# The start of a memory pool moves to a multiple of 256 bytes in a decoder-layer kernel

## The reference, cut to what matters

```
x = x + 0.5 * rmsnorm(swiglu_ffn(rmsnorm(x), w_gu1, w_down1))        # hidden width 2816
u = rmsnorm(x) @ w_in                                                 # four parts of 512
c  = silu(rmsnorm(causal_dwconv31(u_val * sigmoid(u_glu))))
yb = rg_lru(causal_dwconv4(u_x)) * gelu(u_gelu)
x = x + rmsnorm(concat(c, yb) @ w_out)
x = x + 0.5 * rmsnorm(swiglu_ffn(rmsnorm(x), w_gu2, w_down2))
x = x + rmsnorm(sigmoid(rmsnorm(x) @ ple_w_gate) * (p @ ple_w_proj))
```

## Time and profile before

| | |
|---|---|
| median of 3 runs | 2107.99 us (2106.99 to 2108.95) |
| span of the profiled execution, first to last instruction | 2105.4 us (its own time isn't listed) |
| instructions | 34,476, of them 13,041 matmuls |
| busy: TensorE, VectorE, ScalarE, GpSimd | 98%, 56%, 32%, 3% of the span |
| granted TensorE clock, mean | 0.998 |
| moved by DMA | 116.17 MB, 55 GB/s over the span |

### The profile page before, as it was taken

One profiled execution on the slowest core, in us unless ns is written; L12 is line 12 of the kernel. 1 busy time (PEld: TensorE's weight loads), 2 busy tenths in 40 slices (PEclk: granted clock), 3 DMA queues, 4 the chain that ended last, 5 costly groups with the idle time before them and its releaser, 6 DMA issues. The chain is left out here.

```text
span 2105.4 us, 34476 instructions
## 1 busy us (share of the span) xinstructions
PE 2065.3 (98%) x13041; PEld 2049.7 (97%) x13041; DVE 1188.6 (56%) x2367; ACT 681.6 (32%) x1401; POOL 71.7 (3%) x110
## 2 busy tenths in 40 slices
PE   7999999999999999999999999999999999999998
PEld 7999999999999998999999999999999999999997
DVE  5643544354435579537886855345544554358877
ACT  4321222122212234316774532212121222124555
POOL 0000000000000002321000000000000000000000
PEclk9999999999999999999999999999999999999999
DMA  5171111011101102332121211011101110021213
GB/s 166 61 106 35 60 60 40 20 60 60 43 17 60 60 1 50 67 58 50 45 82 61 80 61 61 10 50 60 60 16 44 60 60 30 29 80 41 61 41 103
DMA packets 153277, 116.17 MB, mean 55 GB/s; under 512 B 72648, under 2 KB 143628, under 8 KB 153200
## 3 DMA queue, kind: packets, MB, share of 16 engines
q1 hardware_dynamic: 117728, 108.41, 16.8%
q10 hardware_dynamic: 33424, 5.67, 2.0%
q0 software_dynamic: 2048, 1.06, 0.3%
HBM read 105.96 MB, written 9.15 MB: 55 GB/s over the span
## 5 line engine op out<-in xcount | busy, mean ns | idle before, releaser
L852 PE MATMUL ps<-x_hi,w_lo 128*128 128x352 f32 x2688 | 884.3, 329 | 6.9 <-DVE w_lo L2118 3.0
L854 PE MATMUL ps<-x_hi,w_hi 128*128 128x352 f32 x2688 | 869.7, 324 | 0.0
L853 PE MATMUL ps<-x_lo,w_hi 128*128 128x352 f32 x2688 | 865.2, 322 | 0.0
L852 PEld LDWEIGHTS ps<-x_hi,w_lo 128*128 128x128 f32 x2688 | 505.9, 188 | 10.1 <-issue 4.5
L853 PEld LDWEIGHTS ps<-x_lo,w_hi 128*128 128x128 f32 x2688 | 509.5, 190 | 0.0
L854 PEld LDWEIGHTS ps<-x_hi,w_hi 128*128 128x128 f32 x2688 | 506.4, 188 | 0.0
L852 PE MATMUL ps<-a_hi,wd_lo 128*128 128x352 f32 x1104 | 358.1, 324 | 6.5 <-DVE a_lo L2223 3.7
L854 PE MATMUL ps<-a_hi,wd_hi 128*128 128x352 f32 x1104 | 357.6, 324 | 0.0
L853 PE MATMUL ps<-a_lo,wd_hi 128*128 128x352 f32 x1104 | 355.6, 322 | 0.0
L2271 DVE TENSOR_TENSOR acc<-ps,acc 128x352 f32<-128x352 f32 x480 | 249.7, 523 | 88.7 <-PE ps L854 80.6
L2206 DVE TENSOR_TENSOR tmp_u<-ps,rstd_pre 128x352 f32<-128x352 f32 x132 | 69.0, 524 | 342.0 <-PE ps L854 342.0
(11 more groups left out here) (226 smaller groups left out, 1567.7 us busy)
## 6 DMA issues: line engine op xcount, KB each, us to landing
raw<-in_ffn_w_gu_dram SPq DMA_DIRECT2D x88, 512.0 KB, 3.5
rawd<-in_ffn_w_down_dram SPq DMA_DIRECT2D x22, 1024.0 KB, 7.3
raw<-in_w_in_dram SPq DMA_DIRECT2D x16, 512.0 KB, 4.0
raw<-in_w_out_dram SPq DMA_DIRECT2D x16, 512.0 KB, 4.0
raw<-in_ple_w_gate_dram SPq DMA_DIRECT2D x16, 512.0 KB, 4.0
toeplitz<-rev ACTq DMA_DIRECT2D x8, 512.0 KB, 8.3
x_in<-in_x_prompt_dram SPq DMA_DIRECT2D x4, 512.0 KB, 10.0
toep_first<-toeplitz SPq DMA_DIRECT2D x32, 64.0 KB, 2.2
```

The source lines that it names most:

```text
L852: eng.matmul(dst, wl, xh, start=first, stop=False)
L853: eng.matmul(dst, wh, xl, start=False, stop=False)
L854: return eng.matmul(dst, wh, xh, start=False, stop=last)
```

## The change

One line: the pool's start, and with it the running offset, is rounded up to the next multiple of 256 bytes. Sizes, order, engines and queues are untouched.

```
         st_out = tile("st_out", [P, NJ, 36])
-        pool0 = at[0]
+        pool0 = at[0] = (at[0] + 255) // 256 * 256

         acc = tile("acc", [P, KT, TOK])
```

## The result

The kernel after takes 2093.53 us (median of 7 runs, 2090.77 to 2102.49), the kernel before beside it 2108.95 us: a ratio of 0.9929, 95% interval [0.9909, 0.9949]. That is faster by 0.7%, where no change was forecast, and more than the largest gain for which the prediction had a price. The profiled spans are 2105.4 and 2091.4 us, 14.0 us apart. Of the seven executions of either kernel two took some 10 us longer than the rest (2118.9 us before, 2102.0 and 2102.5 after), so the medians and the profiles are those of the majority. The instructions, their order and their queues are the same; 44 tiles stand 32 bytes further on.

The account below looks back on a forecast made before the run. TensorE bounds the kernel: number of matmuls times 160 to 161 ns, plus some tens of us of waits. Matmuls, VectorE and ScalarE, and transfers were each taken as 0, giving 2108.0 us, range 2104.5 to 2111.5.

Parts of the forecast that it names:

- Two placements, one pace, chunk by chunk, to 0.2 ns: Feed-forward loop matmuls: activations and tokens, placed differently, both run at 160 to 161 ns, so moving the pool gains 0.
- The bound of 4.2 us: Most the matmuls could gain: 2.3 us from 3312 activation matmuls at the third chunk's pace, 1.9 us from output projection.
- The closing caveat: Prediction fails if pace depends on an address feature both placements share, such as the upper half of a 256-byte stretch.
- the first rival: Head, before the first matmul: transfers into the pool run better, 0.3 to 1.7 us shorter; chance 0.08.
- that hint: Stores of 256 KB land in 2.8 us from the pool, 2.0 to 2.3 from outside, perhaps a price of misalignment.
- The second rival: Only the output projection changes, as y moves against weights outside the pool: up to 1.9 us either way; chance 0.05.
- The third rival: Faster: all moved matmuls reach the best pace, 4.2 us, and the head gains 1.7 us: 2102.1 us; chance 0.06.

Follow-up runs that it names:

- run 1: Kernel before with only activations and down weights moved to multiples of 256 bytes, all else in place modulo 256: 2092.13 us, 0.9916.
- run 9: Kernel before, no address moved; three one-column matmuls added behind the first tile of each activation chunk of a steady loop step: 2135.22 us, 1.0131.
- run 8: Kernel before with only the down weights moved to a multiple of 256 bytes, activations left at 224 past: 2101.77 us, 0.9969.
- run 10: Kernel before with wide weights and what stands behind them moved to put wide weights at 160 past, pool at 0, tokens still at 128: 2114.57 us, 1.0013.
- run 3: Kernel before with the first tile 96 bytes later, so tokens and wide weights stand at 224 past 256 like the unmoved pool: 2100.92 us, 0.9954.
- run 6: Kernel before with the whole pool moved by 64 bytes, to 32 past a multiple of 256: 2107.13 us, 0.9992.
- run 12: Kernel before with activations at 32 and down weights at 128 past a multiple of 256, all else in place: 2107.53 us, 0.9973.
- run 11: Kernel before with activations at 0 and down weights at 32 past a multiple of 256, all else in place: 2106.9 us, 0.9995.
- run 7: Kernel before with only the activations moved to a multiple of 256 bytes, down weights left at 224 past: 2096.36 us, 0.993.

## Why the prediction was wrong

**The step that failed** is "Two placements, one pace, chunk by chunk, to 0.2 ns", from which it took 0 for the matmuls. It read tokens (128 and 0) and activations (224) as two independent samples of what a placement costs. They weren't: the tokens' 161.1 ns in the earlier trace rows were inherited from the seam with the activations, as the 159.2 and 158.9 ns ahead of such a seam, run 1 (tokens faster with no operand of theirs moved) and run 9 (another pace with no address moved) show. In place of the 0 stand 0.82 us a loop step. Equal paces on both sides were a sign of the carry-over, and I read them as a sign that placement doesn't matter.

**The bound of 4.2 us** failed by the same step, twice. It took the best pace in sight as the best there is, the third chunk's 160.0 ns; the loops now have 158.9 ns, which the trace before shows only at the beginning of either block, ahead of 77.67 us and from 1261 to 1292 us. And it counted only the 3312 matmuls on activations, while two thirds of the gain lie in tokens. By the steps of before and after, 0.82 us a step over the equivalent of some 18 steps (14.5 / 0.82) is the gain.

**The closing caveat** named the right family, "an address in a way that the two placements of today happen to share", and the wrong member: the two placements differed in what counts, by 32 modulo 64, and lay in one kernel where each spoiled the other.

**What held.** The clock stays at the upper level in the loops, and VectorE's and ScalarE's groups stay within 1 ns. The first matmul starts at 7.80 in place of 7.88 us, not at the 6.2 of the first rival; the first token matmul comes 0.6 us earlier (16.44 against 17.05), but in run 8, with the staged tokens at 224 as before, it came at 16.45 us, so no effect of alignment can be read from the head. The stores of y_stage landed in 2.4 us after, in 2.7 in run 10, where they stand at 0 as well, and in 2.5 in run 3, where they stand at 224, so that hint was no alignment either. The second rival's mechanism is real (y tiles of 3.89 and 3.92 went to 3.87 and 3.82, because there the disagreement of the two operands vanishes), and its gain went into waits for other work in that stage. The third rival had the sign and the engine right; its size was wrong, as it took the 160.0 ns as the best pace and left the tokens out.

**Why, as far as it is shown.** Shown: the pace depends on the places, modulo 64 bytes, of what TensorE reads in turn, tokens, activations and both sets of weights; if all agree (0, 64, 128 or all at 224), the loops settle at 158.9 ns; where they disagree, a slow pace is kept up from step to step; and a pace outlasts what set it off, be it a seam, a wait (run 3) or a break (run 9). Agreement makes the fast pace possible and doesn't enforce it: some y tiles of after still take 3.87 us, 161 ns. Not shown: what in the chip makes these rhythms, some 1.1 ns apart; why a seam tips the tokens in before and in runs 6 and 12, their first chunk in run 11, and not in runs 7 and 8. Down weights at 16 bytes past were not tried, since tiles are placed in steps of 32.

## What to carry to other kernels

Where matmuls like these set the time, try giving every operand that TensorE reads in turn, moving operands and weights of all stages of a loop, the same place modulo 64 bytes; alignment to 256 is one way to get it. A pair that stays 32 bytes off can cost a part of the gain (run 7 kept 12 us, run 8 seven) or all of it (run 10). Only matmuls of this one type and width were measured here. Before using two groups of instructions in one trace as independent evidence on a cause, cut the trace ahead of the first place where they meet: if the pace changes there, one carries the other's. And a bound taken from the best value in a steady stretch is only the best that this stretch has.

## What the runs showed of the hardware

- One and the same stream of fp32r matmuls of 352 columns runs back to back at 158.9, 160.0 or 161.1 ns at clock 1.00, and at 162 to 163 where weights and moving operand stand 32 modulo 128 apart. The listed weight loads of these groups stay at 187 to 190 ns through all of it.
- A rhythm has a memory: tokens at 159.2 ns up to 77.67 us and at 161 ns afterwards with the same operands; a wait of 6.0 us, with a fall of the clock in it, starts the slow pattern of 161.1, 161.3 and 160.2 ns in a kernel whose operands all agree, for one pass; and a break of three one-column matmuls takes the pace back to 158.9 in two of three chunks. Those three cost some 0.67 us, more than four full matmuls.
- The 512 KB transfers of 128-byte pieces took 9.7 us from a source at 96 past, 7.7 from 32 past and 8.3 from 0. In a single wait of 6.0 us on TensorE the clock fell to the lower level for 6.8 us; a wait of 1.8 us was followed by 3.4 us at that level in after and by none in before.
